# A chunk solver's transposed copies: TensorE products of their own in place of turns of the finished copy

## What is computed

```python
def wkv7_scan(r, w, k, v, a, b):
    def step(state, inp):
        r_t, w_t, k_t, v_t, a_t, b_t = inp
        sa = jnp.einsum('bhij,bhj->bhi', state, a_t)
        state = (state * w_t[:, :, None, :] + sa[..., None] * b_t[:, :, None, :]
                 + v_t[..., None] * k_t[:, :, None, :])
        return state, jnp.einsum('bhij,bhj->bhi', state, r_t)
    ...
    _, y = lax.scan(step, state0, xs)
```

## Time and profile before

| | |
|---|---|
| median of 3 runs | 4982.61 us (4970.0, 4982.61, 4983.43) |
| time of the profiled execution | 4970.0 us |
| its span, first to last instruction | 4968.3 us |
| granted TensorE clock, mean | 0.971 of full speed |
| TensorE matmuls busy | 4634.9 us, 93% of the span |
| VectorE, ScalarE, GpSimd busy | 1731.6, 895.4, 566.4 us |
| the recurrence's loop | from 3584.5 to about 3956 us of the span |

### The profile page before, as it was taken

How to read it: one execution, slowest core, us unless ns; L and a number is a source line. 1 busy time by engine, 2 the same in 40 slices (tenths; PEclk the granted TensorE clock), 3 DMA queues, 4 the chain that set the end, 5 groups by cost and what they waited for, 6 DMA issues and landing times.

```text
span 4968.3 us, 39062 instructions
## 1 busy us (share of the span) xinstructions
PE 4634.9 (93%) x15724; PEld 2492.3 (50%) x15724; DVE 1731.6 (35%) x2610; ACT 895.4 (18%) x1621; POOL 566.4 (11%) x531
## 2 busy tenths in 40 slices
PE   6998799999999999999996899779899989999999
PEld 3445644444444455564443444554499834444444
DVE  4211436333324212332799422443533322222100
ACT  2111412000002112221121211333144310000000
POOL 3000104232210000000011200000021003222000
PEclk9998999999999999999998899889999999999999
DMA  4311000111111000000100010000000111111101
GB/s 182 135 50 43 1 34 26 43 43 42 43 44 37 34 30 11 20 9 26 43 34 34 34 68 34 17 30 33 29 1 1 52 46 65 45 49 43 77 35 57
DMA packets 52207, 208.52 MB, mean 42 GB/s; under 512 B 5824, under 2 KB 7360, under 8 KB 50896
## 3 DMA queue, kind: packets, MB, share of 16 engines
q1 hardware_dynamic: 48384, 174.87, 9.7%
q0 software_dynamic: 3664, 31.41, 1.6%
HBM read 191.58 MB, written 14.68 MB: 42 GB/s over the span
## 4 chain that ended last, share of the span: by engine, by line
PE 86%; DVE 9%; ACT 2%; issue 2%; POOL 1%; DMA 0%; ACTq 0%; POOLq 0%; DVEq 0%; SPq 0%; PEldq 0%
PE bank L183 29%; PE bank L463 23%; PE bank L1993 6%; PE bank L2154 6%; DVE bank L1624 5%; PE bank L1349 2%; PE bank L813 2%; PE bank L1376 1%; PE bank L1380 1%; PE bank L1946 1%; PE bank L1929 1%; PE bank L1398 1%; PE bank L2020 1%; PE bank L1938 1%; PE bank L297 1%
## 5 line engine op out<-in xcount | busy, mean ns | idle before, releaser
L183 PE MATMUL bank<-H,ring 128*128 128x512 f32 x2624 | 1139.8, 596 | 29.7 <-DMA ring<-in_proj 19.4
L183 PEld LDWEIGHTS bank<-H,ring 128*128 128x128 f32 x2624 | 500.8, 191 | 660.7 <-issue 622.3
L183 PE MATMUL bank<-ABC,ring 128*128 128x512 f32 x1328 | 577.2, 595 | 19.4 <-issue 14.9
L183 PEld LDWEIGHTS bank<-ABC,ring 128*128 128x128 f32 x1328 | 251.2, 191 | 335.0 <-issue 326.1
L1624 DVE SCALAR_TENSOR_TENSOR bank<-ABC,params,bank 128x1024 f32<-128x1024 f32 x240 | 309.6, 1290 | 8.4
L2154 PE MATMUL bank<-ABC,ring 128*128 128x512 f32 x704 | 304.1, 595 | 2.6 <-PEq L2142 2.6
L463 PE MATMUL bank<-H,ring 128*128 128x512 f32 x576 | 253.1, 592 | 0.0
L2154 PEld LDWEIGHTS bank<-ABC,ring 128*128 128x128 f32 x704 | 134.3, 191 | 172.4 <-issue 169.0
L463 PEld LDWEIGHTS bank<-H,ring 128*128 128x128 f32 x576 | 109.4, 190 | 137.8 <-issue 137.8
L463 PE MATMUL bank<-X 128*128 128x512 f32 x304 | 136.7, 592 | 0.0
L463 PE MATMUL bank<-H,X 128*128 128x512 f32 x304 | 136.7, 592 | 0.0
(11 more groups left out here) (463 smaller groups left out, 6095.1 us busy)
## 6 DMA issues: line engine op xcount, KB each, us to landing
ABC<-in_ada SPq DMA_DIRECT2D x48, 512.0 KB, 6.3
ring<-in_gu SPq DMA_DIRECT2D x44, 512.0 KB, 4.3
ring<-in_up SPq DMA_DIRECT2D x32, 512.0 KB, 4.3
ring<-in_down SPq DMA_DIRECT2D x32, 512.0 KB, 4.4
ring<-in_conv_in SPq DMA_DIRECT2D x24, 512.0 KB, 4.3
ring<-in_ffn SPq DMA_DIRECT2D x16, 704.0 KB, 4.8
ring<-in_proj SPq DMA_DIRECT2D x16, 512.0 KB, 6.4
ring<-in_dft SPq DMA_DIRECT2D x16, 512.0 KB, 4.0
```

Source lines behind the costliest of these rows:

```text
L183: mm = nc.tensor.matmul(bank[:, 2 * (m % 2) + h, :], ring[:, s % RING, k * P:(k + 1) * P], rhs(k)[:, h * HALF:(h + 1) * HALF], start=(k == ...
```

## The change

After levels 1 to 4 the transposed copy isn't made by turning the finished `inv` any more. `level_inv_t`, the product that level 5 has had, now makes it at every level, and stands right behind `level_inv` of the same level. `turn_inv` is gone. TensorE's order, ScalarE's order and the three step lists move accordingly; bank 0 now holds the transposed copy of levels 1 and 2 (before, that of level 1 alone), bank 5 that of levels 3 to 5 (before, 2 to 5). VectorE's and GpSimd's programs stay.

```diff
             rw_pe = steps("rwkv_tensor", rolling(
-                ("x_in", 0), ("x3_", 1), ("inv_t2_", 1), ("u", 0), ("inv3_", 1), ("state", 0), ("x4_", 1), ("inv_t3_", 1),
-                ("gram", 2), ("inv4_", 1), ("out", 0), ("x1_", 2), ("x5_", 1), ("inv_t4_", 1), ("inv1_", 2),
-                ("inv_t5_", 1), ("x2_", 2), ("inv_t1_", 2), ("bk_turn", 2), ("inv2_", 2), ("v_turn", 2)))
+                ("x_in", 0), ("x3_", 1), ("u", 0), ("inv3_", 1), ("inv_t3_", 1), ("state", 0), ("x4_", 1), ("gram", 2),
+                ("inv4_", 1), ("inv_t4_", 1), ("out", 0), ("x1_", 2), ("x5_", 1), ("inv1_", 2), ("inv_t1_", 2),
+                ("inv_t5_", 1), ("x2_", 2), ("bk_turn", 2), ("inv2_", 2), ("inv_t2_", 2), ("v_turn", 2)))
             rw_act = steps("rwkv_scalar", "eye " + rolling(
-                ("x_in", 0), ("inv_t2_", 1), ("u", 0), ("inv3_", 1), ("ident", 2), ("inv_t3_", 1), ("inv4_", 1), ("out", 0),
-                ("inv_t4_", 1), ("inv1_", 2), ("inv_t5_", 1), ("inv_t1_", 2), ("btok", 2), ("ktok", 2), ("inv2_", 2),
+                ("x_in", 0), ("u", 0), ("inv3_", 1), ("inv_t3_", 1), ("ident", 2), ("inv4_", 1), ("inv_t4_", 1), ("out", 0),
+                ("inv1_", 2), ("inv_t1_", 2), ("inv_t5_", 1), ("btok", 2), ("ktok", 2), ("inv2_", 2), ("inv_t2_", 2),
                 ("vtok", 2)))
...
-            def turn_inv(n, c, b):
-                turned(b, inv[c % 2]).then_inc(*rw_pe.did(f"inv_t{n}_{c}"))
-
...
                     level_x(3, c1, 3)
-                    if c >= 0:
-                        pe.wait_ge(*rw_act.after(0, f"inv_t5_{c}"))
-                    turn_inv(2, c1, 5)
...
                     pe.wait_ge(*rw_dve.after(0, f"x3_{c1}"))
-                    pe.wait_ge(*rw_act.after(0, f"inv_t2_{c1}"))
                     level_inv(3, c1, 4)
+                    level_inv_t(3, c1, 5)
...
                     level_x(4, c1, 3)
-                    turn_inv(3, c1, 5)
...
                     level_inv(4, c1, 4)
+                    level_inv_t(4, c1, 5)
...
                     level_x(5, c1, 3)
-                    turn_inv(4, c1, 5)
...
                     level_inv(1, c2, 1)
+                    level_inv_t(1, c2, 0)
...
                     level_x(2, c2, 2)
-                    turn_inv(1, c2, 0)
...
                     level_inv(2, c2, 1)
+                    level_inv_t(2, c2, 0)
                     turned(2, v_bd).then_inc(*rw_pe.did(f"v_turn{c2}"))
...
             def level(n, c):
                 act.wait_ge(*rw_pe.after(0, f"inv{n}_{c}"))
                 nc.scalar.activation(inv[c % 2], bank_q(1 if n < 3 else 4), ACT.Identity).then_inc(*rw_act.did(f"inv{n}_{c}"))
+                level_t(n, c)
 
             def level_t(n, c):
                 act.wait_ge(*rw_pe.after(0, f"inv_t{n}_{c}"))
-                nc.scalar.activation(inv_t[c % 3], bank_q(0 if n == 1 else 5), ACT.Identity).then_inc(*rw_act.did(f"inv_t{n}_{c}"))
+                nc.scalar.activation(inv_t[c % 3], bank_q(0 if n < 3 else 5), ACT.Identity).then_inc(*rw_act.did(f"inv_t{n}_{c}"))
```

More of the change, by code:

```diff
@@ L2271, in b3_scalar @@
                     nc.scalar.activation(x_in, bank_q(6), ACT.Identity).then_inc(*rw_act.did(f"x_in{c}"))
-                if 0 <= c1 < NCH:
-                    level_t(2, c1)
-                if c >= 0:
                     act.wait_ge(*rw_pe.after(0, f"u{c}"))
@@ L2282, in b3_scalar @@
                 if 0 <= c1 < NCH:
-                    level_t(3, c1)
                     level(4, c1)
@@ L2288, in b3_scalar @@
                                          ACT.Identity).then_inc(*rw_act.did(f"out{c}"))
-                if 0 <= c1 < NCH:
-                    level_t(4, c1)
                 if c2 < NCH:
@@ L2295, in b3_scalar @@
                 if c2 < NCH:
-                    level_t(1, c2)
                     act.wait_ge(*rw_pe.after(0, f"bk_turn{c2}"))
```

## The result

The changed kernel takes 5013.03 us (median of 4 runs, 5011.74 to 5013.07), the kernel before 4981.92 (4 runs, 4970.0 to 4983.43). The ratio of the means is 1.0067, with a 95% interval from 1.0049 to 1.0085: slower by 0.7%. The forecast was 5011.9.

What follows compares the result with a forecast made beforehand. TensorE was taken as saturated in the full rounds. 25.7 us there, 0.7 at the start and 2.9 at the end make 29.3, added to the 4982.6 median for 5011.9 us; range 4994 to 5023.

Steps and rivals of the forecast that it cites:

- The bound: In the full rounds TensorE's own work sets the time: 21.81 us of instructions in a 22.27 us round.
- The price of an exchange: Each product replacing a turn on TensorE costs 0.89 us instead of 0.44; 1.80 us more for a chunk.
- The new waits: In each full round, TensorE waits for masked copies: 0.64 us new, while the old 0.46 disappears.
- The three places: inv3 after x3, inv1 after x1 and inv2 after x2 wait for masked copies: 0.21, 0.21 and 0.22 us.
- Start and end: Loop before and behind the full rounds: 0.7 us more at the start, 2.9 at the end, 3 us allowed either way.
- an earlier rise: At the loop's start, products in place of turns could bring the higher clock level sooner, at most 2 us off.
- Putting the sum on the median: For the whole kernel, 29.3 us is added to the 4982.6 us median, not the profiled 4970.0, giving 5011.9.
- rival 1: On TensorE, waits were the cost and the added work is hidden: about 4974 us against 4982.6; chance 0.03.
- rival 2: On TensorE, a product costs four turns, an extra 1.32 us for each of 64: 5067 us; chance 0.01.
- rival 3: ScalarE's two evictions in a row starve TensorE, another 2 us every full round: 5038 us; chance 0.05.
- rival 4: Rounds are bound by something unseen, such as the chain over the state; no measurable difference; chance 0.02.

Runs made afterwards that it cites:

- e1: The kernel before with its four turns of a chunk replaced by products, each left in the turn's old place; 5001.03 us, ratio 1.0041.
- e3: The kernel before with each of the four turns issued twice into the same bank; 5008.90 us (one run).
- e6: The kernel before, in its order, with products in place of turns at levels 3 and 4 only; 4983.52 us (one run).
- e9: The changed kernel with VectorE turning inv at levels 1 to 4, TensorE's order rearranged for cover, x_in's first product waiting for ktok; 4946.68 us, ratio 0.9935.
- e2: The changed kernel, same order and waits, with inv_t1 to inv_t4 made by four TensorE transposes instead of products; 4981.89 us, ratio 0.9998.
- e5: The changed kernel with two long-met waits, ahead of inv2 and inv3, moved ahead of earlier products; 5012.06 us (one run).
- e7: The kernel before, run again without an edit for a second trace; 4982.48 us (one run).
- e4: The changed kernel with VectorE turning inv in 32 x 32 blocks at levels 1 to 4 instead of TensorE's products; 4967.12 us, ratio 0.9961.

## Why the prediction was right

**The bound.** TensorE busy throughout, so that its number of instructions sets the round: shown by e1, e3 and e6, which add 16, 16 and 8 in different kinds and pay 1.73, 1.65 and 0.81 us a round, and by e9, which has 16 fewer than before and gains 2.14, their 1.76 and nearly all of the waiting.

**The price of an exchange.** 0.45 us for each of 64 was the forecast, 1.80 a round. The changed kernel against e2, whose difference is nothing else, gives 1.82. The engine's price by instruction was right, and so was that nothing hides it.

**The new waits.** The three places were right, their size a little short: 0.20, 0.28 and 0.26 us measured, 0.21, 0.22 and 0.21 forecast. The step was the distance from a masked copy's end to the next load, taken as 0.06 us from a product that has one wait in front of it. inv1 has one too and kept to it (3916.97 - 3916.93, 0.04). inv2 and inv3 have a second, met wait ahead, and for them it was 0.12 and 0.11 (3921.70 - 3921.58, 3929.54 - 3929.43). The rows of before had this distance: inv3 there has met waits ahead too and begins 0.11 us after the eviction that holds it (3759.22 - 3759.11). e5 takes the second waits away, and the round comes to 24.25 us, the forecast's number. That term was worth 0.13 us a round, 1.7 in all.

**Start and end.** The full rounds were put at 25.7 us more and gave 27.4; the end at 2.9 and gave 3.1; the start at +0.7 and gave -0.6, within the 3 us allowed. One trace doesn't settle that last term: e5, whose order is the same, has a start of 45.5 us where the changed kernel has 44.5 and before 45.1, so +0.4 instead of -0.6. And the clock rose earlier for good, which the sum hadn't in it. The changed kernel's weight loads there:

```profile
3602.75 0.97 PEld L1993 LDWEIGHTS bank<-ring,H 128*128 128x128 f32 x8 [1.88 <-DVE H L2491]
3605.19 3.48 PEld L1993 LDWEIGHTS bank<-ring 128*128 128x128 f32 x16 [1.47 <-DVE ring L2471]
3608.55 1.02 PEld L1993 LDWEIGHTS bank<-ring,H 128*128 128x128 f32 x8
```

x1's 8 loads took 0.97 us, at the higher level (1.78 in e5, at the lower), the 16 behind it 3.48, mostly at the lower. All loads are at the higher level from 3608.55 on, 11.6 us after the loop's first. In e5 it is 11.9 us; in the trace of before and in e7 it is 15.4. The forecast had weighed an earlier rise, from products in place of turns, and allowed 2 us for it. The rows tie it to something else, to whether TensorE has work right behind inv1, be it product or turn. e1, with products in the old places, changes level within the 8 loads from 14.7 to 15.8 us, and so does e4 (14.6 to 15.8), which has the new order but nothing in that place; e2, with turns in the new places, changes within the loads from 11.3 to 12.4. The row of e2, whose first load is at 3596.60:

```profile
3607.91 1.20 PEld L1993 LDWEIGHTS bank<-ring,H 128*128 128x128 f32 x8 [0.23 <-ACT ring L2258]
```

Where the rise is late, TensorE's loads are idle for 0.98 us behind inv1 (before, e1, e4). No run changes that gap alone. The sum was 29.3 us and the loop grew by 29.96; it came that close because the full rounds' 1.7 us too little and the start's 1.3 too much nearly cancel, which is luck.

**Putting the sum on the median.** The profiled execution of before was 12.6 us under its median; e7 shows that these came about ahead of the loop, half of them by the end of a stretch with another granted clock. The changed kernel's five executions, the profiled one included, all lie from 5011.74 to 5013.07, so the median was the right base: 4982.6 + 29.3 = 5011.9, measured 5013.03.

**The rivals.** The hidden price (rival 1) would have needed more than 1.80 us of waits in a round; e2 shows what its other half was worth: with equal prices the new order isn't faster even so, since it takes the old waits away and brings its own, 0.29 us more. The price of four turns (rival 2) would have made a round of 27.5 us; it was 24.38. ScalarE's two evictions in a row (rival 3) delayed TensorE by next to nothing: the round's work is 21.81 + 1.80 = 23.61 us, and of the remaining 0.77 the three waits are 0.74. That the round isn't bound by TensorE (rival 4) is refuted by e3.

## What to carry to other kernels

On an engine that is busy in every hundredth of a stage, count its instructions first: removing a wait there is worth what the gaps between start and start add up to (0.46 us a round here), and the work given for it must cost less. To shorten such a stage, move work to an engine with time to spare, by the structure of the data if need be (32 x 32 blocks here), and then look again at what lies behind each product: half of e4's gain was lost to waits until the order gave each copy its cover. Compare the changed stretch between two marks in the traces, not the spans, when the rest of the program differs by more than the effect from run to run.

## What the runs showed of the hardware that was not expected

- A wait that had long been met cost 0.06 us when it stood ahead of the one that held TensorE (1.16 and 1.15 us from start to start in the changed kernel, 1.10 and 1.09 in e5), and nothing behind it (0.05 us from the eviction's end to inv2's load in the kernel before).
- The same program spent 12.5 us more or less ahead of the loop, and the granted clock of one window was 0.91 or 0.81 with it (e7).
- At the loop's start the granted clock's higher level came 11.6 us after the first load where TensorE had work right behind inv1, and 15.4 in the kernel before, where it idled there; a turn in that place (e2) brought it about as early as a product.
- VectorE's transpose of a 128 x 512 float32 tile in 32 x 32 blocks took 0.68 to 0.71 us, no longer than a masked copy of that size.
